# Gated linear layer: the diagonal of the scores summed on VectorE, its keys by tokens made on ScalarE

## The reference, cut to what matters

```
k     = (1 - lb) * sigmoid(-fz)
b     = cumsum(g)                                   # g = log forget, per feature
decay = exp(b[t] - b[s])  for s <= t
A     = einsum('thd,shd,tshd->hts', q, k, decay)
o     = A @ v  + (q * exp(b)) @ S                   # then norm, gate, projection w_out
```

## Time and profile before

| | |
|---|---|
| time of 3 runs | 1825.57, 1825.59, 1825.61 us; median 1825.59 |
| profiled execution | span 1823.9 us from first to last instruction; its time is given as this span alone, and the median of the runs lies 1.7 us above it |
| TensorE | 1809.8 us, 99% of the span, 8959 products |
| VectorE | 1269.9 us, 70%, 1717 instructions |
| ScalarE | 942.8 us, 52%, 1310 instructions |
| the gated layer's score work | 4 groups, the eight diagonal products of the groups at 901.7, 1003.6, 1105.5 and 1207.3 us |

### The profile page before, as it was taken

One profiled execution on the slowest core, in us unless ns is written; L12 is line 12 of the kernel. 1 busy time (PEld: TensorE's weight loads), 2 busy tenths in 40 slices (PEclk: granted clock), 3 DMA queues, 4 the chain that ended last, 5 costly groups with the idle time before them and its releaser, 6 DMA issues.

```text
span 1823.9 us, 24555 instructions
## 1 busy us (share of the span) xinstructions
PE 1809.8 (99%) x8959; PEld 1526.8 (84%) x8959; DVE 1269.9 (70%) x1717; ACT 942.8 (52%) x1310; POOL 37.8 (2%) x116
## 2 busy tenths in 40 slices
PE   8999999999999999999999999999999999999999
PEld 7899998888888888887888888888878888888887
DVE  6676766588557755767887878787776556577764
ACT  4545554455465545636655545554445444565542
POOL 2000000000000004000000000000000000000000
PEclk9999999999999999999999999999999999999999
DMA  8555454668789887575554555544767776555453
GB/s 294 160 178 149 139 174 156 206 180 185 175 153 213 172 178 184 185 241 163 166 181 151 163 182 149 175 154 155 233 176 229 218 219 208 162 161 162 159 167 114
DMA packets 175068, 326.74 MB, mean 179 GB/s; under 512 B 16824, under 2 KB 24912, under 8 KB 174208
## 3 DMA queue, kind: packets, MB, share of 16 engines
q1 hardware_dynamic: 173840, 321.04, 61.3%
q10 hardware_dynamic: 576, 4.19, 0.6%
q0 software_dynamic: 560, 0.26, 0.1%
HBM read 319.68 MB, written 5.77 MB: 178 GB/s over the span
## 4 chain that ended last, share of the span: by engine, by line
PE 97%; DVE 1%; ACT 1%; issue 1%; DMA 0%; DVEq 0%
PE acc L366 28%; PE acc L368 27%; PE acc L367 27%; PE ps L615 2%; PE ps L2847 2%; PE ps L463 1%; PE acc L332 1%; PE acc L333 1%; PE acc L331 1%; PE ps L648 1%; DVE wlo L299 1%; ACT whi L284 1%; PE acc L349 0%; PE acc L350 0%; PE acc L353 0%
## 5 line engine op out<-in xcount | busy, mean ns | idle before, releaser
L299 DVE TENSOR_TENSOR wlo<-wraw,whi 128x1024 fp32r<-128x1024 f32 x579 | 699.1, 1223 | 335.3 <-ACT whi L284 332.5
L284 ACT ACTIVATE whi<-wraw 128x1024 fp32r<-128x1024 f32 x579 | 599.8, 1052 | 362.5 <-PE acc L368 330.2
L366 PE MATMUL acc<-whi,ta_hi 128*128 128x512 f32 x1664 | 659.7, 396 | 4.8 <-DVE wlo L299 2.7
L368 PE MATMUL acc<-whi,ta_lo 128*128 128x512 f32 x1664 | 649.2, 390 | 0.0
L367 PE MATMUL acc<-wlo,ta_hi 128*128 128x512 f32 x1664 | 647.8, 389 | 0.0
L366 PEld LDWEIGHTS acc<-whi,ta_hi 128*128 128x128 f32 x1664 | 312.6, 188 | 71.3 <-issue 4.1
L368 PEld LDWEIGHTS acc<-whi,ta_lo 128*128 128x128 f32 x1664 | 312.3, 188 | 66.7
L367 PEld LDWEIGHTS acc<-wlo,ta_hi 128*128 128x128 f32 x1664 | 312.8, 188 | 62.1
L366 PE MATMUL acc<-whi,tb_hi 128*128 128x512 f32 x576 | 228.2, 396 | 0.0
L368 PE MATMUL acc<-whi,tb_lo 128*128 128x512 f32 x576 | 224.8, 390 | 0.0
L367 PE MATMUL acc<-wlo,tb_hi 128*128 128x512 f32 x576 | 224.4, 390 | 0.0
(11 more groups left out here) (331 smaller groups left out, 1618.1 us busy)
## 6 DMA issues: line engine op xcount, KB each, us to landing
wraw<-in_ml_w_in SPq DMA_DIRECT2D x129, 512.0 KB, 5.9
wraw<-in_a_w_in SPq DMA_DIRECT2D x128, 512.0 KB, 3.8
wraw<-in_kv_w SPq DMA_DIRECT2D x64, 512.0 KB, 4.3
wraw<-in_b_w_in SPq DMA_DIRECT2D x64, 512.0 KB, 4.3
wraw<-in_mla_w_in SPq DMA_DIRECT2D x49, 512.0 KB, 4.6
wraw<-in_mla_w_out SPq DMA_DIRECT2D x32, 512.0 KB, 3.9
wraw<-in_ml_w_out SPq DMA_DIRECT2D x32, 512.0 KB, 4.6
wraw<-in_a_w_out SPq DMA_DIRECT2D x32, 512.0 KB, 4.0
```

Of the source, the lines that this page charges most:

```text
L284: nc.scalar.activation(unit_of(whi, n, SPLIT, w), unit_of(wraw, n, RAW, w), ACT.Copy).then_inc(w_high, 1)
L299: nc.vector.tensor_tensor(unit_of(wlo, n, SPLIT, w), unit_of(wraw, n, RAW, w), unit_of(whi, n, SPLIT, w).bitcast(F32), ALU.subtract).then_ ...
L366: nc.tensor.matmul(o, xh, wh, start=first, stop=False)
L368: m = nc.tensor.matmul(o, xl, wh, start=False, stop=end)
```

## The change

TensorE's eight products `diag` of each group are gone. ScalarE makes the keys a second time, now tokens by features, in place in `fw2` (the projected fz): `token_keys`, exp, ln(1 + ...), exp(-...), at unit 18 + 3. VectorE multiplies them with `qw2` (`product`, unit 19 + 3), sums over the 128 features of each token and head (`product_sums`, unit 19 + 4), and the instruction that fills `aT` now takes the identity times these sums instead of the identity times a product in PSUM. Semaphore `dg` is now counted by VectorE, `tk` is new, `ss` is merged into `v`.

```diff
+        L2_AT = {"turn": 16, "decay": 17, "token": 18, "product": 19, "diag": 21, "level": [23, 25, 27, 29, 31, 33, 35, 37], "gate": 38, "pv": 39,
...
+                def token_keys():
+
+                    act.wait_ge(l2["tf"], 1 + g)
+                    f = fw2.rearrange("p b n -> p (b n)")
+                    nc.scalar.activation(f, f, ACT.Exp).then_inc(l2["tk"], 1)
+                    act.wait_ge(l2["tk"], 1 + 3 * g)
+                    nc.scalar.activation(f, f, ACT.Ln, bias=1.0).then_inc(l2["tk"], 1)
+                    act.wait_ge(l2["tk"], 2 + 3 * g)
+                    nc.scalar.activation(f, f, ACT.Exp, scale=-1.0).then_inc(l2["tk"], 1)
...
+                if u == L2_AT["token"] + LAG:
+                    token_keys()
...
+                def product():
+
+                    dve.wait_ge(l2["tk"], 3 + 3 * g)
+                    f, q = [v.rearrange("p b n -> p (b n)") for v in (fw2, qw2)]
+                    nc.vector.tensor_tensor(f, f, q, ALU.mult).then_inc(l2["dg"], 1)
+
+                def product_sums():
+
+                    dve.wait_ge(l2["dg"], 1 + 2 * g)
+                    if not first(g):
+                        dve.wait_ge(l2["at"], g)
+                    nc.vector.tensor_reduce(qk_sums, fw2.rearrange("p b (h d) -> p (b h) d", d=HD), AX,
+                                            ALU.add).then_inc(l2["dg"], 1)
...
-                    dve.wait_ge(l2["dg"], 1 + g)
-                    nc.vector.tensor_tensor(aT, ps2(0).rearrange("p (n t) -> p n t", t=P),
-                                            ident[:].unsqueeze(1).to_broadcast([P, 8,
-                                                                                P]), ALU.mult).then_inc(l2["at"], 1)
+                    dve.wait_ge(l2["dg"], 2 + 2 * g)
+                    nc.vector.tensor_tensor(aT, ident[:].unsqueeze(1).to_broadcast([P, 8, P]),
+                                            qk_sums.unsqueeze(2).to_broadcast([P, 8, P]), ALU.mult).then_inc(l2["at"], 1)
...
+                if u == L2_AT["product"] + LAG:
+                    product()
+                if u == L2_AT["product"] + LAG + 1:
+                    product_sums()
...
-                def diag():
-                    pe.wait_ge(l2["qT"], 1 + g)
-                    pe.wait_ge(l2["kt"], 1 + g)
-                    for n in range(8):
-                        m = nc.tensor.matmul(ps2(0)[:, n * P:(n + 1) * P], kT2[:, n, :], qT2[:, n, :], start=True,
-                                             stop=True)
-                    m.then_inc(l2["dg"], 1)
```

More of the change, by code:

```diff
@@ L857, in build @@
         dT = A(2, G4)
+        qk_sums = sm[:, 0:8]
         qx, kx = A(2, 2 * T), A(2, 2 * T)
@@ L880, in query_half @@
             return halves(v, h, h, 2 * T - h)
-        l2 = sems(2, "tq tf qT nf lf kx kt ge gs dg at df ee op lv sel pv sq ss v rs on og ogp tmp hi lo back rev masks")
+        l2 = sems(2, "tq tf qT nf lf kx kt ge gs dg at df ee op lv sel pv sq tk v rs on og ogp tmp hi lo back rev masks")
         def dst_l2(name, k, b, it):
@@ L895, in free_l2 @@
                 if not first(it):
-                    eng.wait_ge(l2["tf"], it)
+                    eng.wait_ge(l2["dg"], 2 * it)
             elif k == 2:
@@ L902, in free_l2 @@
                     eng.wait_ge(l2["ogp"], TB * it)
-        L2_AT = {"turn": 16, "decay": 17, "diag": 21, "level": [23, 25, 27, 29, 31, 33, 35, 37], "gate": 38, "pv": 39,
+        L2_AT = {"turn": 16, "decay": 17, "token": 18, "product": 19, "diag": 21, "level": [23, 25, 27, 29, 31, 33, 35, 37], "gate": 38, "pv": 39,
                  "norm": 39, "back": 42}
@@ L1518, in norm @@
                                              ACT.Square).then_inc(l2["sq"], 1)
-                    act.wait_ge(l2["v"], 1 + g)
+                    act.wait_ge(l2["v"], 2 + 2 * g)
                     nc.scalar.activation(sm[:, 40:48], sm[:, 32:40], ACT.Ln).then_inc(l2["rs"], 1)
@@ L2302, in norm @@
                     nc.vector.tensor_reduce(sm[:, 32:40], dT[:, 0, :].rearrange("p (n d) -> p n d", d=HD), AX,
-                                            ALU.add).then_inc(l2["ss"], 1)
-                    dve.wait_ge(l2["ss"], 1 + g)
+                                            ALU.add).then_inc(l2["v"], 1)
+                    dve.wait_ge(l2["v"], 1 + 2 * g)
                     nc.vector.tensor_scalar(sm[:, 32:40], sm[:, 32:40], 1.0 / HD, EPS, ALU.mult,
@@ L2871, in l2_side @@
                     turned()
-                if u == L2_AT["diag"]:
-                    diag()
                 for j in range(8):
```

## The result

The changed kernel takes 1833.48 us (median of 5 runs, 1832.65 to 1833.67) against 1825.59 us (5 runs, 1825.25 to 1825.74): ratio 1.0043, 95% interval 1.0032 to 1.0054. It is slower by 7.9 us; the forecast was 1831.8 us within 1829.5 to 1834.5. The profiled execution took 1833.38 us, with a span of 1831.1 us from first to last instruction.

What follows compares the result with a forecast made beforehand. TensorE, busy 1809.8 of 1823.9 us, was taken as the bound, but VectorE's 2.27 us delay would make it wait: 1.54 + 3 x 1.57 = 6.25 us on 1825.59 gives 1831.8 us, range 1829.5 to 1834.5.

Steps and rivals of the forecast that it cites:

- TensorE's products, 1.79 us a group: Score stages: removing TensorE's eight diagonal products saves 1.79 us a group, 7.2 us over four groups if nothing waits.
- the first rival: Added work is hidden and the products are saved: capped at 2.8 us, 1822.8 us, with VectorE not delayed; chance 7%.
- ScalarE's passes at nothing: ScalarE's three added passes, 1.06 us each, fit into idle time before the splits of units 22 and 23; cost nothing.
- VectorE's 2.27 us ahead of `distance(0)`: Product (1.13 us) and reduction (1.14) go on a gapless VectorE stretch, so `distance(0)` starts 2.27 us later.
- The delay is not made good in the ring: Levels: VectorE's 2.27 us delay persists at every level; TensorE is 1.54 us later at level 6, 1.57 in other groups.
- the ring: VectorE and ScalarE releasing each other through the levels: a round takes 6.36 us, TensorE's round 6.39.
- the head: VectorE's stretch from the scans to `scale(0)`, said to run without a gap, so added instructions delay what follows.
- VectorE's 1.03 us of idle time in a round: In each round of the levels, VectorE's 1.03 us idle is a wait within VectorE's and ScalarE's cycle, no reserve.
- The sum, 6.25 us: Over four groups at level 6, 1.54 + 3 x 1.57 = 6.25 us more: 1825.59 becomes 1831.8 us.
- 0.14 us from release to product: At the levels, 0.14 us passes between VectorE's release and TensorE's product behind it; bounds took none to 0.28.
- The clock, given as a rival with 5%: After level 0's 2.54 us wait, TensorE runs one unit at 1.2 GHz: 2.7 us a group, 1842.7 us; chance 5%.
- a ScalarE that is late: Rival: passes delay unit 22's split over 1.1 us; each further us costs 4 us, with one 1835.8 us; chance 6%.

Runs made afterwards that it cites:

- the last experiment: Changed kernel with ScalarE's passes and VectorE's product, reduction and fill moved into idle time, TensorE's products still removed: 1819.79 us, ratio 0.9969.

## Why the prediction was right, and where it was off

- **TensorE's products, 1.79 us a group.** Right as a length; and, as the prediction said, not worth it here. With nothing added 2.6 us came out of 7.2 (cap of the first rival: 2.8).
- **ScalarE's passes at nothing.** Shown by the kernel with the passes alone, within its interval of 0.1%.
- **VectorE's 2.27 us ahead of `distance(0)`.** Measured 904.94 - 902.65 = 2.29 us in group 0; the trace as a whole runs 0.04 later there, and the two instructions take 1.14 + 1.13 = 2.27. The fill costs the same from SBUF as from PSUM (1.22 us in both traces). By the Trainium skill, "VectorE: DVE Perf Modes", section on the TRN2 errata, it should be 65 ns shorter, an estimate from the page's two fixed costs; this trace doesn't agree.
- **The delay is not made good in the ring.** Shown from both sides: in the changed kernel `scale(0)` ends 2.30 us later than before and `scale(6)` 2.27, and moving the fill off the head brought level 6 forward by nearly as much as `scale(0)` (0.84 and 0.88 us, to 948.04 and 908.75). The prediction called VectorE's 1.03 us of idle time in a round no reserve. That is right for a delay that comes from the head. For work that is put into the idle time itself it isn't: the fill there, and the reduction in the last experiment, cost the ring a few hundredths.
- **The sum, 6.25 us.** With the clock at 1.00 throughout and the products put back, 6.5 us. What is missing is 0.06 us in each group. The prediction took 0.14 us from release to product everywhere; in this kernel's group 0 it is 0.06 at level 0 and 0.17 at level 6, and the next product comes 0.87 behind the start of level 6 instead of 0.81.
- **The clock, given as a rival with 5%.** This is the step that was off. It was no alternative to the forecast, it is a term on top of it, and the sum had it at nothing: its price was one unit at half clock, 2.7 us more in a group, in all four groups or in none. In the profiled execution it came in one group of four, cost 1.6 us between two levels and 0.8 net. Runs whose mean granted clock is 0.998 took 1833.5 to 1833.7 us, the two of 0.999 took 1832.65 and 1833.38; their spans are 1831.7 to 1831.9 us against 1830.8 and 1831.1, a step of the size of one fall's net cost. So most runs probably had two such falls, but only one execution was profiled. Forecast 6.25 + 0.2 for the releases + 0.8 to 1.6 for the clock = 7.3 to 8.1 us, measured 7.9.
- **Where luck had a part.** From its own costs the prediction expected 1831.2 to 1833.1 us, and the measured 1833.48 lies above that. It lies within the stated range because that had been widened for a ScalarE that is late, which it wasn't. That the clock's share fit in there is luck.

When the clock falls stays open in part. The traces show it behind all four waits of 3.5 us and one of four of 2.4 us, and behind none of 1.4 (the fill moved) or 0.5 us. Why the one of group 1 and not the others wasn't settled. The Trainium skill, "TensorE: Matmul & The Clock Gate", section on the gate, says that idleness brings the array to 1.2 GHz and work brings it back; the trace agrees in the two levels (1.00 and 0.50). Idleness alone doesn't tell when: as the prediction applied that rule, all four waits of 2.4 us would have brought a fall, and in the profiled execution one did. The prediction also said that the trace before had only shorter waits. It had a longer one, 5.86 us at the kernel's start, ahead of TensorE's first product, and the granted clock behind it was 1.00.

## What to carry to other kernels

When two engines run in step, the bound engine's saved work is worth only the lead that the other one has at its tightest meeting, and that lead has to be looked up at every meeting of the stage (here 1.66 us at the first, 0.84 at the seventh). An added instruction cost nearly nothing in an idle gap, and on a stretch without one about its distance from start to start (1.13 us here; the fill 0.95, since 0.17 of it hid a wait); look at the stretch and not at the 70% of the page. And a wait on TensorE (2.4 us here in one case of four, 3.5 us in all four) can cost again what the clock loses behind it, so leaving TensorE some work there was no worse than leaving it idle.

## What was not expected of the hardware

With eight products of 128x128 put back in front of a wait, the kernel wasn't slower (1832.05 us with them, 1833.48 without), because the shorter wait didn't bring the granted clock to 0.50. And a fall cost less than the time at half clock suggests: 1.6 us lost directly in group 1, of which 0.8 is left at its end, since TensorE then doesn't wait at the later levels.
